# First norm computed on rows of x and turned by transposes, the bias bands' product moved to the head of TensorE's order, and one transfer in place of two to repeat the bands in memory

## The reference, cut to what matters

```python
h = rmsnorm(x, attn_pre_norm[l])        # x: 256 x 1024
proj = h @ w_in[l]
...
def rmsnorm(x, g):
    y = xf * lax.rsqrt(jnp.mean(xf * xf, axis=-1, keepdims=True) + EPS) * g
...
bias = rel_bias[t5_causal_bucket(dist)]  # swa_sink_attention: one number for each head and distance
s = s * (HEAD_DIM ** -0.5) + bias        # banded: 0 <= dist < 128
```

## Time and profile before

| | |
|---|---|
| median of three runs | 1045.28 us (1044.31 to 1046.72) |
| the profiled execution, device time | 1042.57 us |
| its span in the trace | 1040.8 us |
| PE, PEld busy | 98%, 94% |
| DVE, ACT, POOL busy | 77%, 57%, 16% |
| HBM read, mean | 225.19 MB, 219 GB/s |

### The profile page before, as it was taken

How to read it: one execution, slowest core, us unless ns; L and a number is a source line. 1 busy time by engine, 2 the same in 40 slices (tenths; PEclk the granted TensorE clock), 3 DMA queues, 4 the chain that set the end, 5 groups by cost and what they waited for, 6 DMA issues and landing times.

```text
span 1040.8 us, 19237 instructions
## 1 busy us (share of the span) xinstructions
PE 1024.4 (98%) x7860; PEld 974.9 (94%) x7860; DVE 804.5 (77%) x1378; ACT 592.5 (57%) x1027; POOL 165.4 (16%) x172
## 2 busy tenths in 40 slices
PE   8999999999999999999999999999999999999997
PEld 7988898999889997999999999988999999999997
DVE  5877799999997977588999788885678576674443
ACT  5688676666446766665444455443465566544443
POOL 1000134333102100032212011201100123111010
PEclk8999999999999999999999999999999999999999
DMA  9733356776894433457998787653435546774441
GB/s 364 266 117 123 122 195 243 282 285 248 342 401 146 157 126 118 188 191 275 377 370 308 288 322 271 202 196 127 163 122 186 179 142 235 280 260 148 168 168 41
DMA packets 34132, 227.49 MB, mean 219 GB/s; under 512 B 3795, under 2 KB 4092, under 8 KB 10492
## 3 DMA queue, kind: packets, MB, share of 16 engines
q1 hardware_dynamic: 33596, 223.63, 58.9%
q0 software_dynamic: 448, 2.63, 0.6%
HBM read 225.19 MB, written 2.63 MB: 219 GB/s over the span
## 4 chain that ended last, share of the span: by engine, by line
PE 87%; DVE 9%; ACT 2%; issue 1%; DMA 1%; POOL 0%; SPq 0%; POOLq 0%; ACTq 0%; DVEq 0%
PE psum L1506 21%; PE psum L1508 21%; PE psum L1507 21%; DVE w_lo L2258 3%; PE psum L1571 2%; PE psum L1574 2%; PE psum L1573 2%; PE psum L1922 2%; PE psum L1924 2%; PE psum L1923 2%; PE psum L1713 1%; ACT w_hi L820 1%; DVE arena L2582 1%; PE psum L1868 1%; PE psum L1605 1%
## 5 line engine op out<-in xcount | busy, mean ns | idle before, releaser
L2258 DVE TENSOR_TENSOR w_lo<-raw,w_hi 128x1024 fp32r<-128x1024 f32 (+2 forms) x340 | 387.3, 1160 | 143.5 <-ACT w_hi L820 137.8
L820 ACT ACTIVATE w_hi<-raw 128x1024 fp32r<-128x1024 f32 (+2 forms) x340 | 333.4, 996 | 210.3 <-PE psum L1508 155.7
L1506 PE MATMUL psum<-h_hi,w_hi 128*128 128x256 f32 (+1 forms) x1144 | 324.3, 283 | 5.1 <-DVE w_lo L2258 2.6
L1508 PE MATMUL psum<-h_hi,w_lo 128*128 128x256 f32 (+1 forms) x1144 | 320.1, 280 | 0.0
L1507 PE MATMUL psum<-h_lo,w_hi 128*128 128x256 f32 (+1 forms) x1144 | 319.9, 280 | 0.0
L1506 PE MATMUL psum<-hid_hi,w_hi 128*128 128x256 f32 (+1 forms) x952 | 270.9, 285 | 0.5 <-DVE w_lo L2258 0.4
L1507 PE MATMUL psum<-hid_lo,w_hi 128*128 128x256 f32 (+1 forms) x952 | 268.1, 282 | 0.0
L1508 PE MATMUL psum<-hid_hi,w_lo 128*128 128x256 f32 (+1 forms) x952 | 268.1, 282 | 0.0
L1506 PEld LDWEIGHTS psum<-h_hi,w_hi 128*128 128x128 f32 x1144 | 214.8, 188 | 8.5 <-DVE w_lo L2258 5.1
L1507 PEld LDWEIGHTS psum<-h_lo,w_hi 128*128 128x128 f32 x1144 | 215.7, 189 | 0.7 <-issue 0.7
L1508 PEld LDWEIGHTS psum<-h_hi,w_lo 128*128 128x128 f32 x1144 | 215.2, 188 | 0.0
(11 more groups left out here) (297 smaller groups left out, 1221.2 us busy)
## 6 DMA issues: line engine op xcount, KB each, us to landing
arena<-in_ada SPq DMA_DIRECT2D x48, 1024.0 KB, 6.6
raw<-in_gu SPq DMA_DIRECT2D x44, 1024.0 KB, 6.7
raw<-in_ret_in SPq DMA_DIRECT2D x24, 1024.0 KB, 4.9
raw<-in_up SPq DMA_DIRECT2D x22, 1024.0 KB, 4.9
raw<-in_dn SPq DMA_DIRECT2D x32, 704.0 KB, 4.2
raw<-in_qkv SPq DMA_DIRECT2D x12, 1024.0 KB, 5.0
raw<-in_down SPq DMA_DIRECT2D x11, 1024.0 KB, 7.9
raw<-in_ret_o SPq DMA_DIRECT2D x8, 1024.0 KB, 4.9
```

The lines of the kernel that those rows point to most:

```text
L820: nc.scalar.activation(w_hi[chunk % SPLIT_SLOTS][:, a:b], raw[chunk % RAW_SLOTS][:, a:b], ACT.Copy)\
L1506: nc.tensor.matmul(out, w[0], hc, start=start, stop=False, skip_group_check=True)
L1508: return nc.tensor.matmul(out, w[1], hc, start=False, stop=stop, skip_group_check=True)
L2258: tt(w_lo[s][:, a:b], raw[chunk % RAW_SLOTS][:, a:b], w_hi[s][:, a:b].bitcast(F32), ALU.subtract)\
```

## The change

- x is loaded twice: first by rows (`x_rows`: 128 partitions x 2 x 1024, a row is a token; two transfers of the sizes of before), and by features only with chunk number 4, for its use much later.
- The squares are summed along the rows by ScalarE and VectorE, half a row each, so the sums stand one to a partition and the factor is a column of numbers: no sums by TensorE, no diagonal, no spread. x times factor is formed by rows in four pieces of 128 x 512 (`row_h`), one on ScalarE and three on VectorE.
- TensorE turns these by 16 transposes of 128 x 128 (`turn_x`), two for each tile of `h`. ScalarE takes the high part with the gain straight from PSUM (`round_turned`), VectorE the rest from PSUM too. GpSimd has no part in it.
- `rel` comes with `onehot`, which is loaded before `ident` and `cols`; the band product stands behind 18 products of `keep_busy`, and 4 follow it.
- GpSimd stores the band once, 128 times over, straight from its 8 partitions to `band_rows`, and then reads it back as before.
- The first half of chunk LAT0 is loaded in two quarters. The product of LAT0 has a loop of its own (`first_features`), in which the transposes of the tiles 4 to 7 stand between the products.

```diff
-NORM_GROUPS = [[8], [2, 1], [], [], [], [8], [], [8], [8], [8], [8], [8]]
+NORM_GROUPS = [[], [2, 1], [], [], [], [8], [], [8], [8], [8], [8], [8]]
...
         @block.sync
-            for k in (0, DT // 2):
-                cut = slice(k * S, (k + DT // 2) * S)
-                sp.dma_start(x[:, cut], dram["x"][:, cut]).then_inc(x_in[2 * k // DT], 16)
+            for r in range(2):
+                cut = slice(r * D, (r + 1) * D)
+                sp.dma_start(x_rows[:, cut], dram["x_rows"][:, cut]).then_inc(x_rows_in[r], 16)
+            sp.dma_start(onehot, dram["onehot"]).then_inc(onehot_in, 16)
...
+                    if ph.name == "w_in" and step.j == 4:
+                        sp.dma_start(x[:, :], dram["x"]).then_inc(x_in, 16)
...
             pool.wait_ge(band_ready, 1)
-            pool.dma_start(dram["band"], band).then_inc(band_out, 16)
-            odd_rest(1)
-            odd_rest(3)
+            pool.dma_start(dram["band_repeat"], over(band, P)).then_inc(band_out, 16)
             pool.wait_ge(band_out, 16)
-            pool.dma_start(dram["band_rows"], dram["band_repeat"]).then_inc(band_out, 16)
-            odd_rest(5)
-            odd_rest(7)
-            pool.wait_ge(band_out, 32)
             pool.dma_start(v3(a1["bias"], 8), dram["band_skew"]).then_inc(bias_in, 16)
...
         @block.scalar
+            for r in range(2):
+                act.wait_ge(x_rows_in[r], 16)
+                nc.scalar.activation(row_part(row_h, r, 0), row_part(x_rows, r, 0), ACT.Square, scale=D ** -0.5,
+                                     accum_out=row_stat[:, 28 + r:29 + r]).then_inc(pre_sq, 1)
...
+            def round_turned(k):
+                act.wait_ge(pre_turned, k + 1)
+                nc.scalar.activation(h_hi[:, k * S:(k + 1) * S], turned_x(k), ACT.Identity, scale=col("pre", k)).then_inc(pre_hh, 1)
...
         @block.tensor
-            keep_busy(20)
-            pe.wait_ge(ones_filled, 1)
-            sums(PRE)
-            pe.wait_ge(cols_in, 16)
+            keep_busy(18, lin[1])
             pe.wait_ge(onehot_in, 16)
-            nc.tensor.matmul(tra[0][0:8, 0:BAND], col("rel", 0, 8, BUCKETS + 1), onehot, start=True, stop=True).then_inc(band_ps, 1)
-            keep_busy(6)
-            spread(PRE)
-            keep_busy(8)
+            nc.tensor.matmul(sco[0][0:8, 0:BAND], onehot[:, BAND:BAND + 8], onehot[:, 0:BAND], start=True, stop=True).then_inc(band_ps, 1)
+            keep_busy(4, lin[1])
+            pe.wait_ge(ident_in, 16)
+            def turn_x(k):
+                for r in range(2):
...
+                    ins = nc.tensor.transpose(turned_x(k)[:, r * P:(r + 1) * P], row_h[:, r * D + k * P:r * D + (k + 1) * P], ident[:, :])
+                ins.then_inc(pre_turned, 1)
...
         @block.vector
+            for r in range(2):
+                dve.wait_ge(x_rows_in[r], 16)
+                own = row_part(x_rows, r, 1)
+                ins = nc.vector.tensor_tensor_reduce(row_part(row_h, r, 1), own, own, 1.0 / D, 0.0, ALU.mult, ALU.add,
+                                                     row_stat[:, 30 + r:31 + r])
...
+            for r, n in ((1, 0), (0, 1), (1, 1)):
+                ts(row_part(row_h, r, n), row_part(x_rows, r, n), scales[:, r:r + 1], 1.0, ALU.mult, ALU.mult).then_inc(pre_rows, 1)
...
+                stt(h_lo[:, cut], turned_x(k), col("pre", k), h_hi[:, cut].bitcast(F32), ALU.mult, ALU.subtract).then_inc(pre_tiles, 1)
...
-    dram["band_repeat"] = bass.AP(band, 0, [[0, P], [1, 8 * BAND]])
+    dram["band_repeat"] = bass.AP(rows, 0, [[BAND, 8], [8 * BAND, P], [1, BAND]])
```

More of the change, by code:

```diff
@@ L325, in build, with row_part, turned_x @@
         rt["rot"] = rt["t"][:, 0:2 * S]
-        band, onehot = arena[0:8, 4096:4096 + BAND], arena[0:BUCKETS + 1, 4096 + BAND:4096 + 2 * BAND]
+        x_rows, row_h = e0["sq"], e0["y"]
+        def row_part(of, r, n):
+            return of[:, r * D + n * 512:r * D + (n + 1) * 512]
+        def turned_x(k):
+            return (tra + att + sco[1:])[k % 5][:, 0:S]
+        band, onehot = arena[0:8, 4096:4096 + BAND], arena[0:BUCKETS + 1, 4096 + BAND:4096 + 2 * BAND + 8]
         a1["gate"] = a1["lat"][:, 0:2 * S]
@@ L1649, in bank_free, with features @@
                 return lin[unit % 2]
[L1651 to L1656, removed]
+            def features(ph, c, bank, nb, kt, rhs=(h_hi, h_lo), first_tiles=None, hooks={}, whole=True):
+                whi, wlo = weights(ph.chunk0 + c, Step(c), ph)
                 cut2, blocks, half_at = ph.halves(c)[1][0] // P, nb * kt, 0
@@ L1663, in features @@
                         hooks[n]()
[L1664 to L1667, removed]
+                    at = b * kt + k
+                    if at >= cut2 and half_at == 0:
                         half_at = 1
                         second_half(ph, Step(c))
-                    if first_tiles is not None and b == 0 and odd is not None and k % 2:
-                        pe.wait_ge(odd, k // 2 + 1)
-                    elif first_tiles is not None and b == 0:
+                    if first_tiles is not None and b == 0:
                         pe.wait_ge(first_tiles[0], first_tiles[1] + k + 1)
@@ L1678, in features, with first_features @@
                         ins.then_inc(half_done, 1)
+            def first_features(bank):
+                for k in range(DT):
+                    if 0 < k < 5:
+                        turn_x(k + 3)
+                    t = slice(k * S, (k + 1) * S)
+                    for b in range(2):
+                        at, q = 2 * k + b, k // 2
+                        cut, out = slice(at * P, at * P + P), bank[:, b * S:(b + 1) * S]
+                        if at % 4 == 0:
+                            pe.wait_ge(hi_ready if q % 2 else first_hi, q // 2 + 1)
+                        if b == 0:
+                            pe.wait_ge(pre_hh, k + 1)
+                        nc.tensor.matmul(out, w_hi[0][:, cut], h_hi[:, t], start=at == 0, stop=False, skip_group_check=True)
+                        if at % 4 == 0:
+                            pe.wait_ge(split_ready if q % 2 else first_lo, q // 2 + 1)
+                        nc.tensor.matmul(out, w_lo[0][:, cut], h_hi[:, t], start=False, stop=False, skip_group_check=True)
+                        if b == 0:
+                            pe.wait_ge(pre_tiles, k + 1)
+                        ins = nc.tensor.matmul(out, w_hi[0][:, cut], h_lo[:, t], start=False, stop=at == 2 * DT - 1, skip_group_check=True)
+                        if at in (DT - 1, 2 * DT - 1):
+                            ins.then_inc(half_done, 1)
             def value_rows(c, after):
@@ L1754, in _ @@
             ph = PH["w_in"]
-            features(ph, LAT0, bank_free(0), 2, DT, first_tiles=(h_tiles, 0), odd=odd_tiles)
+            first_features(bank_free(0))
             features(ph, LAT1, bank_free(1), 2, DT)
@@ L2313, in rest_of @@
                         ins = stt(lo_[:, cut], tmp[:, cut], shift(k), hi_[:, cut].bitcast(F32), ALU.add, ALU.subtract)
[L2314 to L2322, removed]
+                    ins.then_inc(h_tiles, 1)
+                scale_tiles(i, rest_of)
             def norm_h(i, meanwhile=None):
@@ L3177, in lay_out @@
         "sinks": np.tile(i["swa_sinks"][0][heads], (P, 1)),
[L3178 removed]
+        "fbias": np.repeat(i["forget_bias"][0], 32)[:, None], "fsel": fsel,
     }
+    arrays["onehot"] = np.concatenate([arrays["onehot"], rel], 1)
     arrays["cols"] = np.concatenate([vectors[n].astype(f32) for n in COLS], 1)
```

114 lines of the change are left out of this document (60 added, 54 removed).

## The result

The changed kernel is slower: 1060.11 us, median of 4 runs (1059.10 to 1060.93), beside 1044.80 (1043.45 to 1046.72) for the kernel before, one run more than ahead of the prediction; the ratio is 1.0146, with a 95% interval of 1.0134 to 1.0158. The forecast was 1042.9, its range 1040 to 1050. The profiled execution took 1059.10 us, with a span of 1057.3, so the two profiled executions are 16.5 us apart.

What follows compares the result with a forecast made beforehand. TensorE was taken as the bound (87% of the chain), with time to gain only at its start. From the median 1045.28, 2.9 us earlier less 0.5 waiting at QA0 gave 1042.9 us; own range 1041.5 to 1044, overall 1040 to 1050.

Steps and rivals of the forecast that it cites:

- First step, the front: Kernel start, up to LAT1's first product: to begin at 19.4 instead of 22.34 us, 2.9 us earlier.
- the kinder clock: TensorE at LAT0: full clock is met early, so LAT1 starts at 17.9 to 18.2, a gain of 4.1 us.
- the first rival: Start and QA0: full clock early, gain 4.1 us, and no wait for QA0's weights; 1041.2 us, chance 0.08.
- Second step, the band and its issue: Band product and copy at the start: band ready and GpSimd's store issued at 8.5 us.
- Third step, the transfers: DMA up to QA0: store takes 4.7 us of all engines, lands at 20.5; TensorE waits 0.5 us at QA0.
- the sentence on the Trainium skill's page: Band store: by about 27 GB/s a port, with partitions 0 to 7 reaching two, it takes some 29 us.
- the last rival: First scores: store limited by its 8 partitions takes 31 us, bias late, TensorE waits 11; 1053.4 us, chance 0.14.
- The third rival: QA0: store on 8 engines at 17 GB/s each delays weights, TensorE waits 5.8 us; 1048.2 us, chance 0.16.
- starves for weights as well: Added clause on the case of late bias: TensorE also lacking weights could make it worse; no size given.
- The second load of x costs nothing: SyncE's queue: the 1.05 MB load, 2.5 us of all engines, delays only ROWS1, so it costs nothing.
- The cover named for it: ROWS1, behind the second load of x, has the longest wait for use; cover gone, the cost would be 2.5 us.
- the last rivals: Two slower cases: store holds QA0's weights back, 1048.2 us, chance 0.16; bias comes late, 1053.4 us, chance 0.14.

Runs made afterwards that it cites:

- late_x: Changed kernel with bands repeated in memory in two steps as before, and the second load of x moved to the first step of w_out: 1040.43 us, 0.9952.
- two_hops: Changed kernel, but the bands go to memory in two steps as before, a 12 KB store and then a memory-to-memory copy: 1043.29 us, 0.9988.
- spread: Changed kernel with its one band transfer sent from 128 partitions instead of 8, and the read back matched to it: 1045.26 us, 1.0008.
- apart4: Changed kernel with the 8 source partitions of the band transfer four apart instead of side by side: 1044.99 us, 1.0014.
- one_port: Changed kernel with bands at partitions 0 to 3 and 32 to 35, sent in two transfers: 1092.88 us, 1.0457.
- two_ports: Changed kernel with bands at partitions 0 to 3 and 64 to 67, sent in two transfers: 1069.77 us, 1.0235.
- act_queue: Changed kernel with its one band transfer issued by ScalarE instead of GpSimd: 1056.77 us, 1.0111.
- after_late_x: Changed kernel, its one band transfer kept, with only the second load of x moved to the first step of w_out: 1061.99 us, 1.0165.
- experiment 6: The run act_queue: changed kernel with its band transfer issued by ScalarE instead of GpSimd, 1056.77 us, 1.0111.
- before_one: Kernel before the change, with only the one band transfer out of 8 partitions put in: 1062.65 us, 1.0178.

## Why the prediction was wrong

**First step, the front: right, undersized.** 2.9 forecast, 3.5 measured. The eight transposes took 1.43 (allowed 1.1 to 2.2), and the lower clock ended within 13 to 14 instead of at 14.4. late_x shows that the gain is real. In five of the ten profiles with this front (two_hops, spread, apart4, one_port, two_ports) the clock stayed at 1.00 from 10 to 15 us, where the changed kernel's has 0.66, and LAT1 began at 17.4 to 18.4: the kinder clock, for which the first rival counted on 17.9 to 18.2, is not rare.

**Second step, the band and its issue: right.** 8.44 against 8.5.

**Third step, the transfers: this failed, by one term.** The store was costed at 4.7 us of all engines and a landing at 20.5, out of a store too small to show a limit (12 KB from the same 8 partitions) and a copy from memory to memory, which has no such source. It took 36.7 us and landed at 45.1. QA0's weights, put at 28.1 to 28.6, landed at 42.5, and TensorE waited 13.4 there instead of 0.5. The nearest prices stood in the sentence on the Trainium skill's page (29 us) and in the last rival (31 us), and the 31 was luck: it is the middle between two bounds, 5.8 and 57, neither of which describes this transfer. What limits it is its source, which no row showed: partitions 0 to 3 and 32 to 35 gave 22 GB/s (one_port, 34 to 44 us), and 0 to 7 gave 43 over the whole transfer.

**What followed from it was wrong twice.** The last rival had the store's pace but let the weights through: bias at 53, a wait of 11, 1053.4. That is act_queue (13.2; 1056.8), not this kernel. The third rival had the weights held, on one engine in two, which fits the share of 0.49, but with a wait of 5.8 us, at 17 GB/s an engine. The kernel does both together: the pace of the one, the victim of the other. Of that the prediction had only the clause that TensorE "starves for weights as well". In the changed kernel the bias cost nothing: VectorE's first scores started at 57.97 without a wait, since everything had shifted.

**"The second load of x costs nothing": wrong by what full engines cost.** With the slow store moving it gained nothing (after_late_x). Without the slow store, moving it turned 1043.3 into 1040.4, of which TensorE's 1.7 us at QA0 are the visible part. The cover named for it, ROWS1's late use, was not the place where it was paid.

**The clock.** The sum of the last rivals left out what a pause costs afterwards: 2.6 us here, on top of 15.5 of waiting.

## What to carry to other kernels

Price a DMA by its slowest side, and look at which partitions it reads and not at its bytes alone: the same 1.57 MB took 14.0 us out of 128 partitions, 23.9 out of 8 scattered ones, 36.7 out of 8 neighbours, and 48.8 and 75.3 out of two times 4 that lie 64 and 32 apart. A slow transfer is no private matter of the one who waits for it: look at what other queues have in flight, and at the GB/s at a full busy share, which fell here from 428 to 293 (15 to 20 us) with the share still at 1.02. Where the DMA engines are full, a shorter front is worth only what its loads allow, and the cheapest thing to give them is to move a load whose use is 100 us away.

## What the runs showed of the hardware that was not expected

**The queue decides whether a slow source hurts others.** At about one pace, a MB of the same transfer occupied the engines 120 us on GpSimd's queue and 43 on ScalarE's (experiment 6). Why the slow source stretches the packets of the one and not of the other is open.

**TensorE has two paces at one granted clock.** Products from 216 to 240 us (count, busy us, mean ns), before and then late_x, all with a granted clock of 1.00 and without idle time:

```profile
L1506 PE MATMUL psum<-h_hi,w_hi 128*128 128x256 f32 x69 | 19.2, 278 | 0.0
```

```profile
L1518 PE MATMUL psum<-h_hi,w_hi 128*128 128x256 f32 x68 | 19.4, 285 | 0.0
```

Their starts follow each other every 117.8 ns before and every 120.0 ns in late_x (means over 9 us). GpSimd's additions in `up`, before and then late_x:

```profile
170.40 0.75 POOL L724 TENSOR_TENSOR arena<-arena 128x256 f32<-128x256 f32 x1 [2.37 <-ACT arena L1175]
...
254.04 0.74 POOL L724 TENSOR_TENSOR arena<-arena 128x256 f32<-128x256 f32 x1 [2.74 <-ACT arena L1175]
```

```profile
166.78 0.74 POOL L733 TENSOR_TENSOR arena<-arena 128x256 f32<-128x256 f32 x1 [2.38 <-ACT arena L1187]
...
251.88 0.74 POOL L733 TENSOR_TENSOR arena<-arena 128x256 f32<-128x256 f32 x1 [2.94 <-ACT arena L1187]
```

The lead shrinks from 3.62 to 2.16: 1.5 us go there, as many as the changed kernel lost after 126 us, and it too had 120.0 there (200 to 280 us). The pace holds for long stretches: the kernel before had 117.8 from 500 to 570 us and two_hops 120.0. But it can change within one: in `up` the kernel before itself went from 120.0 to 117.8 near 165 us, and before_one near 190. Each kernel has one trace, so that the pace differs between runs of one kernel is not shown; I take much of the 3 to 5 us between them to be this, but didn't test it, nor what sets the pace. I would therefore not compare two single executions of this kernel to better than 2 us; the lead at a fixed event near 126 us, ahead of the first such stretch, tells a change of the front better than the end does.
